# Modulation tiles one by one between the attention's projections and the feed forward's products

## The reference, cut to what matters

```python
def modulate(h, shift, scale):
    return h * (1 + scale) + shift

for i in range(DEPTH):
    mod_l = jnp.split((jax.nn.silu(c) @ w_mod[i] + b_mod[i])[:, None, :], N_MOD, axis=-1)
    mod_c = jnp.split((jax.nn.silu(c_ctx) @ w_mod[i] + b_mod[i])[None, None, :], N_MOD, axis=-1)
    h_l = modulate(rms_norm(x, norm1_g[i]), mod_l[0], mod_l[1])
    h_c = modulate(rms_norm(ctx, norm1_g[i]), mod_c[0], mod_c[1])
    ...
    x = x + mod_l[2] * y_l
    x = x + mod_l[5] * squared_relu_mlp(modulate(rms_norm(x, norm2_g[i]), mod_l[3], mod_l[4]),
                                        w_mlp1[i], w_mlp2[i])
```

## Time and profile before

| | us |
|---|---|
| median of three runs | 3950.46 (3945.7 to 3951.65) |
| the profiled execution | 3946.52 |
| its span | 3944.7 |
| busy in the span: PE, DVE, ACT, POOL | 3757.0, 1755.5, 1396.6, 462.9 |
| layer 0's attention, units of groups 0 to 3 | from 120 to 603 |
| layer 0's feed forward | from 659 to 1212 |

### The profile page before, as it was taken

The page is one execution under the profiler, slowest core; times in us unless marked ns, Lnnn a source line. Parts: engine busy times, 40 slices in busy tenths (PEclk is TensorE's granted clock), DMA queues, the critical chain, the costliest instruction groups (busy, mean ns, idle before and its releaser), DMA issues.

```text
span 3944.7 us, 64980 instructions
## 1 busy us (share of the span) xinstructions
PE 3757.0 (95%) x27404; PEld 3355.9 (85%) x27404; DVE 1755.5 (45%) x3158; ACT 1396.6 (35%) x2808; POOL 462.9 (12%) x571
## 2 busy tenths in 40 slices
PE   6999998999998999899999999999997999999998
PEld 5877777888887887788888879999996887999998
DVE  4444465232233455644454463353336545334344
ACT  3444453122123344432322372343233236234232
POOL 1222211000001443100021000010003110011001
PEclk8988989999998999999999999999998999999999
DMA  4022121222233121123221103222221111222222
GB/s 176 33 72 69 53 82 43 97 102 94 96 106 102 60 72 53 65 96 99 94 79 44 49 31 100 86 80 87 92 86 46 46 50 43 94 86 84 92 92 75
DMA packets 88032, 306.07 MB, mean 78 GB/s; under 512 B 9904, under 2 KB 13104, under 8 KB 87616
## 3 DMA queue, kind: packets, MB, share of 16 engines
q1 hardware_dynamic: 84944, 292.72, 21.9%
q0 software_dynamic: 2800, 9.21, 0.7%
HBM read 299.79 MB, written 2.10 MB: 77 GB/s over the span
## 4 chain that ended last, share of the span: by engine, by line
PE 88%; DVE 4%; ACT 4%; DMA 1%; POOL 1%; issue 1%; SPq 0%; DVEq 0%; ACTq 0%; POOLq 0%
PE bank L527 63%; PE bank L589 6%; PE bank L558 2%; PE bank L1008 2%; PE bank L797 2%; PE bank L836 1%; PE bank L681 1%; PE bank L994 1%; PE bank L864 1%; PE bank L742 1%; POOL scratch L2551 1%; PE bank L889 1%; PE bank L876 1%; PE bank L824 1%; PE bank L1130 1%
## 5 line engine op out<-in xcount | busy, mean ns | idle before, releaser
L1772 DVE TENSOR_TENSOR weight_lo<-weight_raw,weight_hi 128x1024 fp32r<-128x1024 f32 (+1 forms) x464 | 560.4, 1211 | 555.3 <-ACT weight_hi L1198 555.2
L527 PE MATMUL bank<-u_hi,weight_hi 128*128 128x256 f32 (+1 forms) x2368 | 685.0, 289 | 8.1 <-DVE u_lo L2491 5.8
L527 PE MATMUL bank<-u_lo,weight_hi 128*128 128x256 f32 (+1 forms) x2368 | 672.4, 284 | 0.0
L527 PE MATMUL bank<-u_hi,weight_lo 128*128 128x256 f32 (+1 forms) x2368 | 671.6, 284 | 0.0
L1198 ACT ACTIVATE weight_hi<-weight_raw 128x1024 fp32r<-128x1024 f32 (+1 forms) x464 | 476.8, 1031 | 526.8 <-PE bank L527 371.0
L527 PE MATMUL bank<-h_hi,weight_hi 128*128 128x512 f32 (+1 forms) x1360 | 500.1, 368 | 18.6 <-DVE h_lo L2193 9.2
L527 PE MATMUL bank<-h_lo,weight_hi 128*128 128x512 f32 (+1 forms) x1360 | 479.6, 353 | 0.0
L527 PE MATMUL bank<-h_hi,weight_lo 128*128 128x512 f32 (+1 forms) x1360 | 479.0, 352 | 0.0
L527 PEld LDWEIGHTS bank<-u_hi,weight_hi 128*128 128x128 f32 x2368 | 448.6, 189 | 34.5 <-issue 28.1
L527 PEld LDWEIGHTS bank<-u_hi,weight_lo 128*128 128x128 f32 x2368 | 448.6, 189 | 0.0
L527 PEld LDWEIGHTS bank<-u_lo,weight_hi 128*128 128x128 f32 x2368 | 447.2, 189 | 0.1
(11 more groups left out here) (272 smaller groups left out, 6954.8 us busy)
## 6 DMA issues: line engine op xcount, KB each, us to landing
weight_raw<-in_w_mlp SPq DMA_DIRECT2D x128, 512.0 KB, 3.5
weight_raw<-in_w_ff SPq DMA_DIRECT2D x128, 512.0 KB, 3.4
weight_raw<-in_w_in SPq DMA_DIRECT2D x92, 512.0 KB, 3.4
weight_raw<-in_w_mod SPq DMA_DIRECT2D x80, 512.0 KB, 3.9
weight_raw<-in_a_w_qkv SPq DMA_DIRECT2D x24, 512.0 KB, 4.3
weight_raw<-in_b_w_qkv SPq DMA_DIRECT2D x24, 512.0 KB, 3.5
first_weight<-in_w_mod SPq DMA_DIRECT2D x16, 512.0 KB, 14.7
weight_raw<-in_w_ret_o SPq DMA_DIRECT2D x16, 512.0 KB, 3.4
```

The lines of the kernel that those rows point to most:

```text
L527: m = e.matmul(view[:, 0:hi - lo], a[:, k, :], b[:, k0 + k, lo:hi], start=(k == 0 and i == 0), stop=(k == kt - 1 and i == 2))
L1772: e.tensor_tensor(wlo[s][:, 0:kt, :], raw[n % N_RAW][:, 0:kt, :], whi[s][:, 0:kt, :].bitcast(F32), ALU.subtract).then_inc(*tick("dve_split ...
```

## The change

The order within a pair of modulation tiles is now tile, turn of the rows of the pair before, tile; ACT's copy for a pair stands at the first tile of the next pair. In the attention's groups 0 to 2 a modulation piece is laid behind every 1/12.5 of the projections' cost; in group 3 two pieces come first and the others are laid into the output product, one per 1/10.5 of its cost. In the feed forward the 73 calls for pieces are spread over 56 products. Residual additions wait for the last tile of the vector that they use (23 or 47).

```diff
+def beside(main, side, every):
+    due = 0.0
+    for cost in main:
+        yield cost
+        due += cost
+        if due >= every:
+            due -= every
+            yield from itertools.islice(side, 1)
+    yield from side
+
+def paced(side, pieces, turns):
+    done = 0
+    for i in range(turns):
+        while done * turns < (i + 1) * pieces:
+            next(side, None)
+            done += 1
+        yield
...
                 if g < 3:
-                    fill = Fill(3 * n + 1, heads_cost(layer) + cost, heads(g + 1), itertools.islice(side, 12))
+                    fill = Fill(3 * n + 1, heads_cost(layer) + cost,
+                                beside(heads(g + 1), itertools.islice(side, 12), heads_cost(layer) / 12.5))
                 else:
-                    fill = Fill(3 * n + 1, KT * product_cost(q_tokens(layer), 6) + cost, splits(), side, output())
+                    out = KT * product_cost(q_tokens(layer), 6)
+                    fill = Fill(3 * n + 1, out + cost, splits(), itertools.islice(side, 2),
+                                beside(output(), side, out / 10.5))
...
-                    if m0 > m_from:
-                        turn_rows(m0 - 2)
-                    yield 0.2
+                        if i == 0:
+                            if m0 > m_from:
+                                turn_rows(m0 - 2)
+                            yield 0.2
                 turn_rows(m_to - 2)
...
                 return mlp(("mlp", layer), H_HI, H_LO, HID, q_tokens(layer), edge(layer), f"w_mlp1_{layer}",
-                           f"w_mlp2_{layer}", normed(("n2", layer)), side2)
+                           f"w_mlp2_{layer}", normed(("n2", layer)), paced(iter(side2), 73, 56))
...
             def modulation(layer, m_from, m_to):
-                for m0 in range(m_from, m_to, 2):
-                    for i in range(2):
-                        split_ahead(number[f"w_mod{layer}", m0 + i])
-                        yield 0.7
+                def copy(m0):
                     e.wait_ge(*at("modp", layer, m0 + 1))
                     e.wait_ge(*(at("modq", layer, m0 - 2) if m0 else at("modq", layer - 1, 46)))
                     e.activation(ROWS, view_of("mod", layer, m0)[:, 0:2 * P], ACT.Copy).then_inc(
                         *tick("act_mod", ("rows", layer, m0)))
-                    yield 0.2
+
+                for m0 in range(m_from, m_to, 2):
+                    if m0 > m_from:
+                        copy(m0 - 2)
+                    for i in range(2):
+                        split_ahead(number[f"w_mod{layer}", m0 + i])
+                        yield 0.7
+                        if i == 0:
+                            yield 0.2
+                copy(m_to - 2)
...
-                e.wait_ge(*at("modd", layer, 47))
+                e.wait_ge(*at("modd", layer, KT * v + KT - 1))
```

More of the change, by code:

```diff
@@ L1520, in diffusion_layer @@
                 mlp(("mlp", layer), HID, q_tokens(layer), edge(layer), f"w_mlp1_{layer}", f"w_mlp2_{layer}", finish,
-                    side2)
+                    paced(iter(side2), 73, 56))
             def hybrid_layer(layer):
@@ L1945, in modulation @@
                         yield 0.7
-                    if m0 > m_from:
-                        add_bias(m0 - 2)
-                    yield 0.2
+                        if i == 0:
+                            if m0 > m_from:
+                                add_bias(m0 - 2)
+                            yield 0.2
                 add_bias(m_to - 2)
```

## The result

The changed kernel takes 3991.69 us in the median (3989.91 to 3992.16), the kernel before 3949.96 beside it. The ratio is 1.0109, with a 95% interval from 1.0096 to 1.0121: slower by 1.1%, some 42 us. I had forecast 19 us less. The profiled execution of the changed kernel has a span of 3988.1 us, 43.4 more than that of before.

The account below looks back on a forecast made before the run. PE, busy 95% of 3944.7 us, was taken as the bound. Attention +35 and feed forward -16 give 19 us less: 3928 from the profiled 3946.52, 3932 for the median, the forecast; range 3908 to 3951.

Parts of the forecast that it names:

- Tiles inside products ... Cost taken as nothing: Attention groups 0 to 2: two tiles between two weights cost 0; at the other end 14 us in all.
- I add 3 for small waits and low clock: Attention groups: 3 us for mid-group waits and low clock, between 0 and 8.4, making 114 us per group.
- the 6: Attention group 0: 6 us gained, from 6.6 us lost today in its row of tiles.
- rival B: Attention gains half, low clock and small waits coming from the groups' own short units: 3949 us, no difference; chance 0.14.
- the gain of 6: Attention group 3: 9 us lost in place of 15.6, so 6 gained, between 1 and 11.
- Forecast -16: Feed forward as a whole: 14.9 us gained less 31.3 lost, so 16 us lost.
- The four waits: Feed forward, w1 phases: a product behind two tiles waits 3.4 us for its weight's split, four times, 13.6 us.
- the three at 2.05: Feed forward, w1 phases: a turn of rows waits 2.05 us for ACT's copy, three times, 6.2 us.
- the one in a w2 phase: Feed forward, pairs 5-6: one wait for a weight's split behind a residual and a split, 0.7 us.
- the clock behind them: Feed forward: 1.7 us lost behind each 3.4 us wait, half that behind each 2.05 us wait; 9.4 us (0 to 20).
- the 14.9 gained: Feed forward: 12.7 us from the end row and 2.2 from the first products behind it are won.
- C: Feed forward: the clock stays low after each wait as around a row, 14 us each; slower, 3971 us; chance 0.05.

Follow-up runs that it names:

- short hold: The changed kernel, but each modulation tile takes its own bank and gives it back once ACT has copied its 128 columns: 3922.52 us, ratio to before 0.9927.
- long hold: The changed kernel itself, where a pair keeps one bank from its first tile to its turn of rows: 3991.69 us, ratio to before 1.0109.
- The withheld bank: The kernel before, with one of eight PSUM banks kept out of use while the heads of group 1 are projected, inside group 0: 3957.41 us, one run.
- the kernel with this part alone: The changed kernel with Fill's list of before in the attention, the paced feed forward and the new pair order kept: 3971.95 us, ratio to before 1.0049.
- The kernel by turns: The changed kernel, but feed-forward products are followed alternately by tile A, then by the turn of rows and tile B: 3959.05 us, ratio to before 1.0025.

## Why the prediction was wrong

**The step that failed** is "Tiles inside products ... Cost taken as nothing" together with "I add 3 for small waits and low clock", under groups 0 to 2. I put this term at nothing, and the small waits at 3 us a group, because I looked at the three raw buffers for what a spread tile holds up and not at the eight banks. A modulation pair takes a bank with `take` and gives it back in `turn_rows`; I followed the waits and DMAs of the moved pieces, but not what they hold while they are spread. What the runs showed in its place: PE waits for banks. The price of the inside is 16.1 us in group 0 (short hold against long hold), 16.7 and 16.6 in groups 1 and 2, so 49 us in all. The case with all eight banks is nearly what I had forecast: 112.5 and twice 117 where my terms give 109.6 (115.6 less the 6) and twice 114, so some 3 us a group are left over.

**The clue was in the rows.** I read group 0's 101.7 us at clock 1.00 and group 1's 0.90 and, in rival B, put group 1's excess down to "the groups' own short units". But the units are the same; what differs inside the group is a bank, held from one row to the next. The withheld bank showed that.

**Group 3.** The wait of the turn of rows for ACT's copy behind six head splits came as worked out from the earlier trace rows: 4.6 us forecast, 4.54 measured. Of the gain of 6 there came 0.7 (112.6 to 111.87). With a short hold the stage takes 104.2, 7.7 less than in the change. There the wait of 4.54 is gone, and so are the waits for `weights_T`, 3.3 us in all in the change. So the banks have a part in what is missing; how much, with the clock behind either, no kernel here parts.

**The feed forward.** Forecast -16, measured -21, in the change as in the kernel with this part alone. The four waits were worked out at 3.4 and are 3.6 to 3.7, the three at 2.05 and are 2.04, the one in a w2 phase and the last one as forecast. Together the waits are 22.9 us, 21.9 forecast. The term that was mis-sized is the clock behind them: 9.4 forecast, and 27.3 us at half clock are 13.7 lost. With the 14.9 gained that makes 22 lost. The kernel by turns agrees: it is 33 us faster than the change, the seven waits are 21 of that, and some 12 are left. I had given the 2.04 us waits half a fall each, and each has a whole one. The Trainium skill (TensorE: Matmul & The Clock Gate, "HAM oscillation — how this bites in real kernels") has the loss of clock paid at each recurring wait, in a case with waits of some 3 to 5 us. The change's trace agrees for the four waits of 3.6 to 3.7 us, and shows the same for the three of 2.04, which are shorter than the page's. Not every such wait has it, though: behind the one of 2.79 us at 1295.98 the clock is 1.00.

**The rivals.** B and C named the right sign of my errors with wrong mechanisms. B had the attention gain half, with short units as the reason; it lost 24 us. C had the clock stay low for long behind each wait; it is back within 6 us of the end of each. The true one, a resource that a spread piece keeps, wasn't on the list. So 0.94 stood on "not slower". The end of group 0 at full clock and the waits of the feed forward came as I had written under what would show it, and neither says anything about the banks.

## What to carry to other kernels

When pieces of work are moved from a block to single places between other work, count what each holds from its start to its end (a PSUM bank, a buffer, a semaphore's turn), and not only what it waits for. In this kernel it paid to let the side job give its bank back at each step, at the price of a second copy. And when a product waits for an engine whose result it doesn't read, look whether that engine empties the bank that the product takes.

Side work between matmuls also needs what it waits for to be done in time. Here that took the tile and the step that depends on it behind different products, and no two unsplit tiles between two weights (or a look-ahead that isn't cut short by them).

## What the runs showed that I had not expected

- One bank of eight, withheld for some 107 us, costs 6.6 us in one run, although no wait there is longer than 0.8. PE has 1.9 us of new waits, and the clock over 120.7 to 229.0 is 0.97 (a stretch of 6.8 us at half).
- With thirteen waits of 0.4 to 1.3 us inside group 0 of the change, the mean granted clock is 0.93 over 128.6 us: three stretches at half clock, 17 us in all. The low clock costs as much as the waits (8.3 against 7.3 us).
- Letting ACT and DVE split one place further takes 3.5 us off a group when banks are short (133.2 to 129.7) and 0.6 when they aren't.
